# Attention maxima and exponentials over two score banks at once, in a Trainium2 encoder kernel

## What is computed

```python
s = jnp.einsum('bqhd,bkhd->bhqk', qn_i, kn) + jnp.einsum('bqhr,bkr->bhqk', qr_i, kr)
p = jax.nn.softmax(s.astype(jnp.float32), axis=-1).astype(v.dtype)
return jnp.einsum('bhqk,bkhd->bqhd', p, v)
```

## Time and profile before

| what | value |
|---|---|
| median of 3 runs | 3202.27 us (3198.29 to 3203.3) |
| profiled execution, its own time | 3200.24 us |
| profiled execution, its span in the trace | 3198.1 us |
| attention | from about 839 to 1507 us of the span |
| TensorE busy over the whole span | 95% |

### The profile page before, as it was taken

One profiled execution on the slowest core, in us unless ns is written; L12 is line 12 of the kernel. 1 busy time (PEld: TensorE's weight loads), 2 busy tenths in 40 slices (PEclk: granted clock), 3 DMA queues, 4 the chain that ended last, 5 costly groups with the idle time before them and its releaser, 6 DMA issues.

```text
span 3198.1 us, 48240 instructions
## 1 busy us (share of the span) xinstructions
PE 3047.8 (95%) x17492; PEld 2561.4 (80%) x17492; DVE 1379.7 (43%) x2447; ACT 1181.4 (37%) x2106; POOL 652.5 (20%) x612
## 2 busy tenths in 40 slices
PE   4899999889899999998999999999999999999999
PEld 4668888678788888887887888888888888877887
DVE  5267777656567666765325211122222222222111
ACT  3462245455355555554325211133323323322111
POOL 2111111067222221221320001011112112113221
PEclk8999999989999999999999999999999999999999
DMA  6233355487211111211652311121211212134331
GB/s 224 73 116 107 101 161 163 153 240 222 65 53 53 53 53 43 60 55 50 214 184 102 119 73 49 63 69 59 79 59 62 76 59 79 52 122 155 105 105 53
DMA packets 259119, 318.53 MB, mean 100 GB/s; under 512 B 17011, under 2 KB 187251, under 8 KB 256020
## 3 DMA queue, kind: packets, MB, share of 16 engines
q1 hardware_dynamic: 258998, 316.89, 30.4%
HBM read 214.07 MB, written 102.76 MB: 99 GB/s over the span
## 4 chain that ended last, share of the span: by engine, by line
PE 85%; POOL 4%; issue 3%; DVE 3%; ACT 3%; DMA 2%; SPq 0%; POOLq 0%; DVEq 0%; ACTq 0%
PE PS L349 12%; PE PS L350 11%; PE PS L351 11%; PE PS L2213 4%; PE PS L2214 4%; PE PS L2215 4%; PE PS L2364 4%; PE PS L2366 4%; PE PS L2365 4%; PE PS L1664 3%; PE PS L1686 2%; PE PS L1687 2%; PE PS L1688 2%; PE PS L2525 2%; PE PS L1653 2%
## 5 line engine op out<-in xcount | busy, mean ns | idle before, releaser
L349 PE MATMUL PS<-hTh,whi 128*128 128x512 f32 x1664 | 659.4, 396 | 26.7 <-DVE hTl L302 14.5
L350 PE MATMUL PS<-hTl,whi 128*128 128x512 f32 x1664 | 650.4, 391 | 0.0
L351 PE MATMUL PS<-hTh,wlo 128*128 128x512 f32 x1664 | 650.4, 391 | 0.0
L349 PEld LDWEIGHTS PS<-hTh,whi 128*128 128x128 f32 x1664 | 314.2, 189 | 100.0 <-issue 14.0
L351 PEld LDWEIGHTS PS<-hTh,wlo 128*128 128x128 f32 x1664 | 314.0, 189 | 66.3
L350 PEld LDWEIGHTS PS<-hTl,whi 128*128 128x128 f32 x1664 | 314.5, 189 | 63.1 <-issue 0.2
L341 POOL TENSOR_TENSOR whi<-wraw,zero 128x1024 fp32r<-128x1024 f32 x52 | 99.8, 1919 | 1202.8 <-PE PS L351 951.0
L1759 ACT ACTIVATE pb__145<-PS,nm,rq 128x512 f32<-128x512 f32 x256 | 197.5, 779 | 129.8 <-DVE nm L1821 129.8
L2213 PE MATMUL PS<-ow_h,of_h 128*128 128x512 f32 x576 | 225.0, 391 | 7.5 <-DVE oy L2168 7.5
L2214 PE MATMUL PS<-ow_l,of_h 128*128 128x512 f32 x576 | 224.8, 390 | 0.0
L2215 PE MATMUL PS<-ow_h,of_l 128*128 128x512 f32 x576 | 224.7, 390 | 0.0
(11 more groups left out here) (256 smaller groups left out, 5961.1 us busy)
## 6 DMA issues: line engine op xcount, KB each, us to landing
projT<-pev SPq DMA_DIRECT2D x80, 256.0 KB, 2.6
xt<-x SPq DMA_DIRECT2D x8, 2048.0 KB, 9.5
mw<-wmod SPq DMA_DIRECT2D x64, 256.0 KB, 2.8
oxt<-x SPq DMA_DIRECT2D x32, 512.0 KB, 4.8
sg_v<-vev SPq DMA_DIRECT2D x64, 256.0 KB, 2.4
wraw<-wuz SPq DMA_DIRECT2D x32, 512.0 KB, 6.0
vm<-sg_v SPq DMA_DIRECT2D x16, 1024.0 KB, 5.6
sgT<-mT SPq DMA_DIRECT2D x16, 1024.0 KB, 4.4
```

The source lines that it names most:

```text
L349: pe.matmul(PS[:, bank, :], w[1][:, s, k, :], hTh[:, k, b], start=(k == 0), stop=False)
L350: pe.matmul(PS[:, bank, :], w[1][:, s, k, :], hTl[:, k, b], start=False, stop=False)
L351: mm = pe.matmul(PS[:, bank, :], w[2][:, s, k, :], hTh[:, k, b], start=False, stop=(k == KD - 1))
```

## The change

The maxima and the exponentials take two banks in one instruction of 1024 columns, so a tile has two of each in place of four. The maximum of a pair waits for the second bank's scores. An exponential releases both banks at its end (its semaphore rises by 2). The last maximum and the last sum are then taken of two numbers by a tensor_tensor in place of a reduce of four. On DVE, `lo(0)` moves ahead of the first maximum, and in the step of u = 0 `lo(2)` moves ahead of the second. TensorE's stream is not edited.

```diff
                 if b == 0:
                     act.wait_ge(s_nm, N * 6 + 6)
                     act.wait_ge(s_T, N * 4 + 4)
-                act.activation(pb_[:, u, blk(b)], PS[:, b, :], ACT.Exp, bias=nm[:, u:u + 1],
-                               scale=rq2[:, 0, ds(i * 2 + u, 1)], accum_out=rs4[:, u, b:b + 1]).then_inc(s_exp, 1)
+                act.activation(pb_[:, u, b * 512:(b + 2) * 512], PS[:, b:b + 2, :].rearrange("p b f -> p (b f)"), ACT.Exp,
+                               bias=nm[:, u:u + 1], scale=rq2[:, 0, ds(i * 2 + u, 1)],
+                               accum_out=rs4[:, u, b // 2:b // 2 + 1]).then_inc(s_exp, 2)
...
                         exps(N, i, u, 0)
-                        exps(N, i, u, 1)
                         piece(2)
                         exps(N, i, u, 2)
-                        exps(N, i, u, 3)
                     else:
                         piece(1)
                         exps(N, i, u, 0)
                         hi(2)
-                        exps(N, i, u, 1)
                         piece(2)
                         exps(N, i, u, 2)
                         hi(3)
-                        exps(N, i, u, 3)
...
             def maximum(N, i, u, b):
-                dve.wait_ge(s_S, N * 4 + b + 9)
-                dve.tensor_reduce(mx4[:, u, b:b + 1], PS[:, b, :], AX, ALU.max).then_inc(s_nm, 1)
-                if b == 3:
+                dve.wait_ge(s_S, N * 4 + b + 10)
+                dve.tensor_reduce(mx4[:, u, b // 2:b // 2 + 1], PS[:, b:b + 2, :].rearrange("p b f -> p (b f)"), AX, ALU.max
+                                  ).then_inc(s_nm, 2)
+                if b == 2:
                     dve.wait_ge(s_nm, N * 6 + 4)
-                    dve.tensor_reduce(mx1[:, u:u + 1], mx4[:, u, :], AX, ALU.max).then_inc(s_nm, 1)
+                    dve.tensor_tensor(mx1[:, u:u + 1], mx4[:, u, 0:1], mx4[:, u, 1:2], ALU.max).then_inc(s_nm, 1)
...
-                dve.tensor_reduce(rsm[:, u:u + 1], rs4[:, u, :], AX, ALU.add).then_inc(s_rinv, 1)
+                dve.tensor_tensor(rsm[:, u:u + 1], rs4[:, u, 0:1], rs4[:, u, 1:2], ALU.add).then_inc(s_rinv, 1)
...
+                    lo(0)
                     maximum(N, i, u, 0)
-                    lo(0)
-                    maximum(N, i, u, 1)
                     lo(1)
                     piece(0)
-                    maximum(N, i, u, 2)
                     if u == 0:
                         lo(2)
                         piece(1)
-                        maximum(N, i, u, 3)
+                        maximum(N, i, u, 2)
                         lo(3)
                         piece(2)
                     else:
                         piece(1)
-                        maximum(N, i, u, 3)
+                        maximum(N, i, u, 2)
```

## The result

The changed kernel took 3213.01 us (median of 7 runs, 3207.63 to 3215.26) beside 3201.39 us of the kernel before on the same chip (7 runs): a ratio of 1.0036 [1.0025, 1.0047]. The profiled execution took 3210.09 us, with a span of 3208.1.

The account below looks back on a forecast made before the run. The PE was taken to bound the attention; 10.3 + 0.5 - 2.0 + 1.3 + 0.2 = 10.3 us on the profiled 3200.24 gave 3210.5, and 2.0 more for the median 3212.5 us. Range 3204 to 3219.

Parts of the forecast that it names:

- the ends: First two handovers and end of the attention: 1.3 us more for both handovers, 0.2 us more at the end.
- The chain: Loop handover u = 0 to u = 1: later maximum and exponential, release 1.425 us behind its start; PE stands 0.33 us.
- The reserve: Loop handover u = 0 to u = 1: bank 0 free at 916.31, matmul at 916.71, 0.40 us to spare.
- The cost of a stall: Loop handover to u = 1: 0.33 us wait plus 0.08 lost weight-load overlap, 0.41 us a pair, 25 times, 10.3 us.
- Given back: Turn 2 in steps of u = 0: `lo(0)` moved ahead saves 0.12 us, 17 times, -2.0 us.
- Pieces: Three pairs with pieces: over a microsecond of PE work ahead of the handover, so nothing is added.
- clock: Rival, second handover: longer wait lowers the PE's clock, about 2 us more, 3214.5 us; chance 0.08.
- Busy time: ACT and DVE in the profile after: both less busy, DVE by about 17 us.
- No stall: Rival, loop handover: chain has 0.33 us more room than counted, 3202 us, not slower; chance 0.12.
- two for two: Rival: a two-bank instruction costs as much as two, 0.51 us more at each of 30 handovers, 3228 us; chance 0.06.
- faster: Rival: ACT and DVE pace the stage, so ACT's saving of 0.7 us a tile gives 45 us, 3157 us; chance 0.04.

Follow-up runs that it names:

- The halves alone: Kernel before with only the exponentials over two banks: 3195.48 us, ratio 0.9988; with only the maxima over two banks and DVE's new order: 3202.22 us, 1.0009.
- the split exponential: Changed kernel with the first exponential of a step of u = 0 in two of 512 columns: 3199.67 us, 1.0003 to the kernel before.
- the copies: Extra ACT copies between `nm` and the first exponential, in several kernels; one of 128 columns in the kernel before, at u = 0: 3203.93 us, 1.0015.
- the copy in u = 0 and in u = 1: Changed kernel plus a 128-column ACT copy between `nm` and the first exponential: 3214.98 us in steps of u = 0, 3212.70 us in steps of u = 1.
- the one that adds a copy to it: Kernel before with only the exponentials over two banks, plus a 128-column ACT copy ahead of the first exponential at u = 0: 3194.81 us, 0.9986.

## Why the prediction was right, and what was off

The forecast was 3212.5 us, and it came out at 3213.01. The step that decides is that the wide exponential and the wide maximum together add more to the chain than the handover from u = 0 to u = 1 has to spare. The halves alone, the split exponential and the copies show it. Two of the prediction's terms were off and nearly cancelled, and so did some of the ends; that the total fits to half a microsecond is luck.

- **The chain.** Foreseen: last maximum 0.50 behind scores 3 (913.67 - 913.17), exponential 2.44, matmul 3.86. Seen: 0.52, 2.49, 3.84. The exponential came 0.05 later than foreseen, and the release 1.35 behind it and not 1.425. By the prediction's own words (wrong "if its release comes faster than 1.43 us behind its start") this term failed. The width was sized rightly: it adds 0.43 us (0.92 to 1.35 in the loop, 1.01 to 1.44 in the handovers that are written out; the instruction itself grew from 0.78 to 1.21). What was mis-sized is the base. The 1.01 us of the earlier trace rows come from a handover that is written out, where the matmul starts 0.23 behind the exponential's end. In the loop it starts 0.14 behind it.
- **The reserve.** The prediction measured it to the matmul (3.54), but the weight load wants the bank at 3.42. So the handover of the earlier trace rows had 3.42 - 3.05 = 0.37 us to spare. That the prediction has 0.40 comes of two errors of about 0.1 that go opposite ways. The change adds 0.36 + 0.43 = 0.79 there, 0.42 more than the reserve. In the median handover of the kernel before, 0.24 are to spare and 0.66 are added, which is 0.42 beyond it again, because the new chain hangs on scores 3 and `lo(2)` and not on where the old one stood.
- **The cost of a stall.** 0.41 us foreseen (0.33 of stand, 0.08 of overlap); 0.30 and 0.10 seen in the rows, and 0.41 in the stretches (19.36 against 18.95). 25 of them make 10.3 us, as foreseen. At the three starts of heads it is 0.23 each (19.17 against 18.95), against 0.17.
- **Given back.** Waits of turn 2, foreseen at 2.0: they were 25 times 0.10 = 2.5 us, and they are gone. The edit that was to do it, `lo(0)` ahead, took 3.8 of 5.2 us of these waits by itself; the exponentials over two banks alone take all of them.
- **Pieces.** I had put nothing on the three pairs with pieces, since their work covers the handover. That was wrong: two pieces wait longer there, in the changed kernel both for DVE's `kvl`. In one such pair of before and of the changed kernel:

```profile
1027.33 0.50 PE L1552 MATMUL PS<-ckh,wkh 128*128 128x512 f32 x1 [0.15 <-DVE kvl L1571]
1033.62 0.50 PE L1552 MATMUL PS<-ckh,wkh 128*128 128x512 f32 x1 [0.19 <-ACT pb__145 L1759]
```

```profile
1030.87 0.50 PE L1552 MATMUL PS<-ckh,wkh 128*128 128x512 f32 x1 [0.28 <-DVE kvl L1571]
1037.40 0.50 PE L1552 MATMUL PS<-ckh,wkh 128*128 128x512 f32 x1 [0.45 <-DVE kvl L1571]
```

 The two waits sum to 0.39 us more, 1.2 us in three pairs if the others are alike (27.2 to 27.6 us for the two stretches that can be read).
- **The ends.** From the first scores to the first shares 2.1 us more, where I had 1.3. The waits of the first two handovers grew by 1.08 (2.22 to 3.30) and 1.09, each more than the 0.95 foreseen, and the stretch shows 0.1 given back where I had counted on 0.6. The lower clock behind the second is what the rival *clock* had described, but what it cost isn't settled. The same stretch took 43.1 us in the changed kernel and 43.0 with the copy in u = 0 and in u = 1, where no scores behind that handover are slow and one of the two waits is longer by 0.14 to 0.15. From the last but one to the last shares 1.1 us less, where I had 0.2 more. That stretch took 16.6 to 20.7 us in the twelve kernels of the experiments, with a granted clock in 1480:1500 from 0.74 to 1.00, so its difference can't be put down to the change.
- **Busy time.** DVE was to be less busy by about 17 us, and the page has 7. The maxima took 18.4 us less, summed one by one (174.2 to 155.9), but DVE's instructions also overlapped less (94.6 us in place of 107.3).
- **The rivals.** *No stall* is refuted by 25 waits, *two for two* by 1205 and 1217 ns, *faster* by a loop pair whose mean fell below 18.95 us in no kernel. In the loops ACT's and DVE's savings gave the 0.10 us a pair of the turn's waits and no more.

The section Optimizing Scalar/DVE Operations of Perfetto Trace Analysis in the Trainium skill, by which breaking up instructions that cause bubbles while their engine isn't saturated may let work finish sooner, fits here: splitting one exponential of the four in a pair of tiles took the loss of the loops away. But it holds for that instruction alone. The other three exponentials of a pair of tiles may be wide, and the kernel with all of them wide and single maxima is, with the one that adds a copy to it, the fastest of the study (0.12% and 0.14% below the one before). That is at the edge of what a measurement tells, and the two can't be told apart.

Where that kernel gains its 3.9 us can be read in part. In its profile the loops are 2.6 us shorter (the turn's waits), each of the two stretches with pieces that can be read 0.5 (26.69 against 27.2 us), and the first stretch 0.7 longer. The last stretch is 2.9 us shorter (16.6 us), with a granted clock of 1.00 in 1480:1500 against 0.83. How much of that is the clock and how much the edit stays open.

## What to carry to other kernels

Where one engine is the bound and others have slack on average, look up the few places where the bound engine takes over a buffer, and write down for each the time at which it is released and the time at which it is wanted. Take the time at which the bank is wanted from the weight load and not from its matmul, and the time of a release from a handover of the same kind, in the loop or written out. An edit that makes instructions wider pays there with the whole added latency beyond the reserve. What it saves in busy time was worth nothing here at that place. Then follow the delay once around the loop: a step that is late by 0.6 us with room at its own handover can come back through another engine's queue at the next.

## What the runs showed of the hardware

- An exponential out of PSUM takes 779 ns for 512 columns and 1205 for 1024, a maximum 681 and 1217. An ACTIVATION_READ_ACCUMULATOR takes about 0.2 us behind each, and the next exponential starts 0.09 us behind the accumulator's start: two wide ones are 1.20 apart, two single ones 0.76 to 0.77.
- The release in a loop handover reached TensorE 1.35 us behind the start of a wide exponential (1.33 with a copy ahead of it) and 0.92 behind that of a single one, both 0.14 behind its end. In the handovers that are written out it was 1.44 and 1.01, both 0.23 to 0.24 behind the end.
- In a loop handover without a wait the weight load of the first matmul stood at 3.42 and the matmul at 3.54. With a release at 3.58, 3.84 and 3.94 the 22 stretches of the loops took 0.16, 0.41 and 0.51 us more than 18.95: the distance from 3.42, and not from 3.54. Of this 0.10 us shows as the second matmul 0.33 behind the first in place of 0.23.
- Behind a wait of 1.34 us at the second handover the scores' matmuls went on at 0.40 us (three kernels). With waits of 1.82 to 2.43 us there, some of the scores' matmuls that followed took 0.63, the lower of TensorE's two clock levels, in nine kernels. Two others, the changed one with a copy, had 2.42 us (u = 0) and 2.57 us (u = 1) and no such matmul. So the length of the wait alone doesn't decide it.
